# Expert weight loads that wait for the landing of the load three places ahead

## What is computed

```
def moe_swiglu(h, router, w1, w3, w2):
    logits = (h @ router).astype(jnp.float32)
    top_v, top_i = lax.top_k(logits, TOP_K)
    probs = jax.nn.softmax(top_v, axis=-1)
    gate = jnp.sum(jax.nn.one_hot(top_i, N_EXPERTS, dtype=jnp.float32) * probs[..., None], axis=-2)
    out = jnp.zeros(h.shape, jnp.float32)
    for e in range(N_EXPERTS):
        out = out + gate[..., e:e + 1] * swiglu(h, w1[e], w3[e], w2[e]).astype(jnp.float32)
    return out.astype(h.dtype)
```

## Time and profile before

| | us |
|---|---|
| median of 3 runs | 2490.42 |
| lowest and highest | 2488.22, 2502.24 |
| the profiled execution | 2504.0 |
| its span in the profile | 2502.2 |

### The profile page before, as it was taken

The page is one execution under the profiler, slowest core; times in us unless marked ns, Lnnn a source line. Parts: engine busy times, 40 slices in busy tenths (PEclk is TensorE's granted clock), DMA queues, the critical chain, the costliest instruction groups (busy, mean ns, idle before and its releaser), DMA issues. The chain is left out here.

```text
span 2502.2 us, 105337 instructions
## 1 busy us (share of the span) xinstructions
PE 2418.6 (97%) x46610; PEld 2015.9 (81%) x46610; DVE 1280.6 (51%) x3333; ACT 607.6 (24%) x1798; POOL 0.2 (0%) x4
## 2 busy tenths in 40 slices
PE   9999999999999999999999999999999999999987
PEld 8987666666699999998765666678999989888876
DVE  7566666666686776666575666677311111111111
ACT  2233333433311100233333333421111111111111
POOL 0000000000000000000000000000000000000000
PEclk9999999999999999999999999999999999999989
DMA  6334432222343454343343222236779999999986
GB/s 249 128 137 151 164 121 91 81 82 74 103 152 135 156 177 145 121 142 140 122 162 131 80 79 77 84 133 245 283 286 365 403 381 389 409 373 393 409 319 270
DMA packets 142657, 496.81 MB, mean 199 GB/s; under 512 B 18400, under 2 KB 23136, under 8 KB 139904
## 3 DMA queue, kind: packets, MB, share of 16 engines
q1 hardware_dynamic: 142336, 492.24, 53.5%
HBM read 471.88 MB, written 20.29 MB: 197 GB/s over the span
## 5 line engine op out<-in xcount | busy, mean ns | idle before, releaser
L306 PE MATMUL psum<-hT,ring 128*64 128x144 f32 (+1 forms) x4568 | 458.3, 346 | 3.4 <-DVE hT L2468 1.7
L306 PEld LDWEIGHTS psum<-hT,ring 128*64 128x64 f32 x4568 | 294.2, 137 | 95.1 <-issue 11.0
L2992 DVE TENSOR_TENSOR work<-psum,work 128x88 f32<-128x88 f32 (+3 forms) x176 | 42.4, 241 | 368.4 <-PE psum L2661 368.1
L2661 PE MATMUL psum<-work,ring 128*64 128x88 f32 (+3 forms) x5120 | 191.9, 234 | 10.2 <-issue 9.4
L2661 PEld LDWEIGHTS psum<-work,ring 128*64 128x64 f32 x5120 | 184.2, 138 | 15.3 <-issue 13.9
L1794 ACT ACTIVATE work<-psum 128x256 f32<-128x256 f32 (+4 forms) x320 | 104.1, 362 | 349.8 <-PE psum L1705 84.8
L306 PE MATMUL psum<-work 128*64 128x144 f32 (+4 forms) x2096 | 155.6, 283 | 4.3 <-DVE work L1285 3.6
L306 PE MATMUL psum<-y_ret,work 128*64 128x144 f32 x2400 | 156.2, 286 | 0.7 <-DVE y_ret L550 0.7
L306 PEld LDWEIGHTS psum<-y_ret,work 128*64 128x64 f32 x2400 | 148.7, 137 | 1.0 <-issue 1.0
L306 PEld LDWEIGHTS psum<-work 128*64 128x64 f32 (+2 forms) x2096 | 122.3, 136 | 31.1 <-issue 11.5
L2983 DVE TENSOR_TENSOR xT<-xT,psum 128x288 f32<-128x288 f32 x64 | 29.1, 455 | 229.4 <-PE psum L2701 228.4
(11 more groups left out here) (528 smaller groups left out, 4175.5 us busy)
## 6 DMA issues: line engine op xcount, KB each, us to landing
ring<-w_ff_dram SPq DMA_DIRECT2D x272, 512.0 KB, 8.2
ring<-w_mix_dram SPq DMA_DIRECT2D x256, 512.0 KB, 3.9
proj<-w_ff_dram SPq DMA_DIRECT2D x96, 512.0 KB, 9.8
lora_w<-w_ff_dram SPq DMA_DIRECT2D x64, 512.0 KB, 7.0
hT<-w_ff_dram SPq DMA_DIRECT2D x64, 512.0 KB, 7.3
y_ret<-w_ff_dram SPq DMA_DIRECT2D x64, 512.0 KB, 8.0
merged<-w_ff_dram SPq DMA_DIRECT2D x32, 512.0 KB, 10.6
work<-s_gla_dram SPq DMA_DIRECT2D x8, 1024.0 KB, 5.1
```

The lines of the kernel that those rows point to most:

```text
L306: last = nc.tensor.matmul(out[64 * c:64 * c + 64], weights[:, 64 * c:64 * c + 64], x, start=start, stop=stop)
L2661: last = mm(up_ps(s, cap)[64 * h:64 * h + 64], up_slot[s][:, k, 64 * h:64 * h + 64], hg[:, k, 0:cap], start=(k == 0), stop=(k == KT - 1))
L2992: tt(hid[:, f, 0:cap], up_ps(2 * f + 1, cap), act1[:, f % 2, 0:cap], ALU.mult).then_inc(sig("up_used"), 2)
```

## The change

In front of the wait for its place and its issue, each load gets a second wait: for the landing of the load three places ahead of it in SP's order (`UNDER_WAY = 3`), which may be one of the expert before. `landed` finds that load's semaphore and the count that it has to reach; for down places 4 and 9, whose semaphore is shared with the next place, it returns without a wait, and the load three places on goes out without one. `load_up` and `load_down` become one function. A `settle` (an increment of a semaphore that nobody waits for) stands between the two waits. `mixed_fills` moves up unchanged, since SP now uses it as PE does. What is loaded, its order, its places and all work of PE, ACT and DVE stay.

```diff
+        UNDER_WAY = 3
...
-            def load_up(p, e, n):
-                sp.wait_ge(slab_done, count(p, EX_SLABS, FF0 + n - EX_RING + 1 - (EX_DOWN if n < EX_RING else 0)))
-                sp.dma_start(up_slot[n % EX_RING], w_ff[e, n]).then_inc(up_in[n % EX_RING], 16)
-
-            def load_down(p, e, d):
-                sp.wait_ge(slab_done, count(p, EX_SLABS, FF0 + UP_SLABS + d - EX_RING + 1
-                                            - (UP_SLABS if d < EX_RING else 0)))
-                sp.dma_start(down_slot[d % EX_RING], w_ff[e, UP_SLABS + d]).then_inc(down_in[d % EX_RING], 16)
-
-            for n in range(EX_RING, UP_SLABS):
-                load_up((0, 0), 1, n)
-            for d in range(EX_RING, EX_DOWN):
-                load_down((0, 0), 1, d)
+            def landed(p, j):
+
+                if j < UP_SLABS:
+                    s, turn = j % EX_RING, j // EX_RING
+                    earlier = mixed_fills(s - 6) if s >= 6 else 0
+                    sp.wait_ge(up_in[s], count(p, UP_TURNS * 16, (earlier + turn + 1) * 16))
+                else:
+                    s, turn = (j - UP_SLABS) % EX_RING, (j - UP_SLABS) // EX_RING
+                    if s in DOWN_SHARED:
+                        return
+                    both = 2 if s in DOWN_SHARED.values() else 1
+                    earlier = mixed_fills(s - 1) if 6 <= s < 9 else 0
+                    nth = earlier + (turn + 1) * both
+                    sp.wait_ge(down_in[s], count(p, DOWN_TURNS * both * 16, nth * 16))
+
+            def load(i, done, e, j):
+
+                if j >= UNDER_WAY:
+                    landed((i, done), j - UNDER_WAY)
+                elif done:
+                    landed((i, done - 1), j - UNDER_WAY + EX_SLABS)
+                p = i, done
+                settle(sp)
+                if j < UP_SLABS:
+                    s = j % EX_RING
+                    sp.wait_ge(slab_done, count(p, EX_SLABS, FF0 + j - EX_RING + 1 - (EX_DOWN if j < EX_RING else 0)))
+                    sp.dma_start(up_slot[s], w_ff[e, j]).then_inc(up_in[s], 16)
+                else:
+                    s = (j - UP_SLABS) % EX_RING
+                    sp.wait_ge(slab_done, count(p, EX_SLABS, FF0 + j - EX_RING + 1
+                                                - (UP_SLABS if j < UP_SLABS + EX_RING else 0)))
+                    sp.dma_start(down_slot[s], w_ff[e, j]).then_inc(down_in[s], 16)
+
+            for j in itertools.chain(range(EX_RING, UP_SLABS), range(UP_SLABS + EX_RING, EX_SLABS)):
+                load(0, 0, 1, j)
...
-                for n in range(UP_SLABS):
-                    load_up((i, 1), e, n)
-                for d in range(EX_DOWN):
-                    load_down((i, 1), e, d)
+                for j in range(EX_SLABS):
+                    load(i, 1, e, j)
```

More of the change, by code:

```diff
@@ L10 @@
+import itertools
 from contextlib import ExitStack, contextmanager
@@ L2549, in up_ps, with mixed_fills @@
             return bank[UP_BANKS[n % EX_RING % len(UP_BANKS)]][:, 0:cap]
+        def mixed_fills(s):
+            return fills_before(layer, s) + fills(len(STREAM), s)
         def column_of(v, n):
@@ L2644, in gather_tokens @@
                     last.then_inc(sig("hg_ps"), 1)
-            def mixed_fills(s):
-                return fills_before(layer, s) + fills(len(STREAM), s)
             def up(p, cap, s, turn):
```

## The result

| | before | after |
|---|---|---|
| median, us | 2496.33 (4 runs) | 2696.90 (4 runs) |
| lowest and highest | 2488.22, 2514.48 | 2693.36, 2698.90 |
| span of the profiled execution | 2502.2 | 2693.5 |

The ratio is 1.0791, with a 95% interval from 1.0726 to 1.0856: slower, and by more than twice what was forecast. The median lies above the top of the range (2661). Most executions of the kernel before lie near 2489 us and some near 2503 us, the profiled one of 2504.0 among these; against a step of 190 us this does not matter.

What follows compares the result with a forecast made beforehand. In the later experts DMA and PE were both taken as near their limits. 456 x 1.51 + 6 x 6.6 = 728.2 us against 634.8 is +93.4, less 5.6 gives +88: 2578 us, 8 in 10 from 2484 to 2661.

Steps and rivals of the forecast that it cites:

- The form of the sum: In the experts, 462 slab landings: 456 at pace P and six at 6.6 us, 728.2 us against 634.8.
- P = 1.51: Forecast us per slab landing in the experts with three under way, the mean of 1.46 and 1.57.
- the two stretches of the earlier trace: 1916 to 1930 and 1829 to 1844 us, about four loads under way: 335 and 358 GB/s, 1.57 and 1.46 us a slab.
- Nearer to the upper row than the lower one: Placed the experts' pace, 1.51 us a slab, between a lower bound of 1.2 and an upper of 1.70.
- The reaction: SP's time from the landing of load j-3 to the issue of load j, estimated at 0.2 us.
- the bound of 1.70: Upper bound of the experts' pace, from one load landing after 4.9 us: (4.9 + 0.2)/3 = 1.70 us a slab.
- worse still: Rival: experts' pace at 1.70 us a slab, +171, 2661 us; top end of the slower case (0.70), holding little of it.
- The jumps: SP's loop jumping back at six expert borders: the queue runs dry, 6.6 us between two landings each, 39.6 in all.
- The tail: From last slab landing to end of the down products: 7.1 us now, some 1.5 needed, giving back 5.6 us.
- Three are enough: Rival: experts' queue stays full at 1.28 us a slab, 0 to 10 us added, 2490 to 2500 us; chance 0.13.
- The short queue frees the instruction loads: Rival: PE code comes sooner in the experts, half of 37.7 us of "issue" waits gone, 2476 us; chance 0.17.
- The sign posts: Trace signs in the experts: near 350 GB/s, landings 4 to 4.5 us, SP waiting on landings, PE idle about 5 us per jump.

Runs made afterwards that it cites:

- the half slabs: The changed kernel with two under way and each experts' load fetching only half its slab (256 KB): 2617.99 us, ratio 1.0511 to the kernel before.

## Why the prediction was wrong

**What bounds the kernel** was right. The PE with slabs at hand was not the limit, the added instructions on SP cost nothing beyond the turn (twelve under way shows it), and the loss is in the landings of 462 slabs.

**The form of the sum** was right too: a turn of landing and reaction, a third of it a slab, six jumps, and a PE that hides behind. With measured terms it is 456 x 1.747 + 28.7 = 825.3 us; this comes out by the way in which the pace is defined, and the test of the turn is that (4.94 + 0.30) / 3 gives the same 1.747.

**The step that failed** is the choice of the pace: P = 1.51, measured 1.747. It is 456 x 0.237 = 108 us of a miss. Three things are in it:
- The landing time with two others ahead. By P = 1.51 and 0.2 us of reaction it would be 4.3 us; it is 4.94. The difference, 0.61 / 3, is 0.20 of the 0.237. The right number was on record: the earlier trace rows, the only row with exactly the state that the change makes, said 4.9 us. I took it as an upper bound, from one load, and went by the two stretches of the earlier trace rows instead, because these showed ten loads on end. But they showed four under way (3.5 and 3.9 in the mean, worked out from the trace; in the changed kernel it is 2.8), and four have a pace of their own: 1.446 measured here, beside the 1.46 and 1.57 of these stretches. They would have done better as a forecast for UNDER_WAY = 4.
- "Nearer to the upper row than the lower one" was argued from bounds of which the lower could not be reached: 3.4 us is the landing of a load alone, and with two others under way it took 4.94. What adds these 1.5 us stays open: if only the bytes at 410 GB/s were shared, three would have been enough (last section).
- The reaction. 0.2 us was an estimate; it is 0.30 (median 0.295), and a `settle` and a second wait stand behind the wait for the landing. That is 0.033 of the 0.237, 15 us. With both ahead of that wait it is 0.15.

So also the bound of 1.70 was no bound: with the right reaction it is (4.9 + 0.30) / 3 = 1.73, and the rival "worse still", priced at 2661, would have been near 2676. It was the case that happened, and the range ended at its price, with no room for the terms in it.

**The jumps** were put at 6.6 us each, 39.6; they took 3.8 to 6.2, 28.7 in all, which gave back 10.9 us. In the one at 2196 us the issue of the expert's last two loads ended at 2196.4, and the next load was issued at 2201.98:

```profile
2194.41 1.95 SPq L2594 DMA_DIRECT2D merged<-w_ff_dram  x2
2201.98 1.01 SPq L2589 DMA_DIRECT2D lora_w<-w_ff_dram  x2
```

5.6 us, where it had been 7.2; over the six, 5.5 to 6.8 from issue to issue against 7.2 to 7.9. Why the jump itself is shorter was not tried. That the queue runs dry at each is right: at all six the last load had landed 0.5 to 2.0 us before the next was issued, and the one issued at 2201.98 landed after 3.26 us, somewhat sooner than the 3.6 of the one that found the queue empty in the earlier trace rows.

**The tail** was to give back 5.6 us and gave 3.1; the start, left out, cost 4.0, as the last loads of the first expert already waited.

**In sum,** +93.4 was forecast for the landings, +108.1 for the pace and -10.9 for the jumps come to it, which makes +190.6. The measured one is +190.5. So the miss is one of size, in the pace, and not of mechanism.

**The rivals.** "Three are enough" needed a landing in 3.6 us with two ahead; it took 4.9, so it is out. The Trainium skill ("DMA: Bandwidth & Descriptors", section "Anatomy of one DMA — SWDGE (gpsimd) path") gives about 2.0 us plus the bytes at 436 GB/s, for another issuing path than SP's, from which 3.2 us for a slab is an estimate. The trace agrees with it for a load alone (3.26 us in the chain), and not with others under way (4.2, 4.9, 5.4 and 6.1 us with two to five). "The short queue frees the instruction loads" did not show in any time, as told above. "Worse still" is what happened.

**The sign posts.** GB/s near 350 was wrong (292), a landing of 4 to 4.5 us wrong (4.9), SP waiting for landings and a chain of DMA pieces right. The PE idle for about 5 us at each jump was right only in part: around the six it idles for 2.9 to 5.5 us in all, mostly in two or more pieces, and only once for over 5 us in one. The PE's clock did fall more often: 0.94 from 2000 to 2100, where it had been 1.00; nothing of it is needed in the sum, since the landings alone account for it.

## What to carry to other kernels

Transfers from one queue whose number is limited by a wait run at number / (landing time + reaction), as long as that wait is the one that binds, and the landing time has to be that with just so many under way, not that of a load alone and not that of a full queue; for the 512 KB loads of this kernel five of them, 2.5 MB, reached the full rate (409 GB/s from 2225 to 2270 us), and with six no loss could be told any more. Where one row of a trace shows exactly the state that a change makes, its number goes into the sum, even if it is one load, and longer evidence from a neighbouring state goes into the range. And a range that ends at a rival's price needs room for the rival's own terms.

## What the runs showed of the hardware that was not expected

- The landing time of a 512 KB load rises slowly with the number under way: about 3.3 us alone (3.26 at a jump), 4.2 with two, 4.9 with three, 5.4 with four, 6.1 with five, 7.1 with six. In a queue that is full throughout each further load would add the 1.28 us of its bytes at 410 GB/s; the steps are 0.9, 0.7, 0.5, 0.7 and 1.0. So part of each transfer, some 1.6 us by the half slabs, runs beside the others without filling the engines. One piece of it shows in the changed kernel's trace: at the six jumps, with nothing else under way, the first packet starts 1.0 to 1.1 us after the issue. But if such a part were all, and the engines gave full rate behind it, three under way would land in 3 x 1.28 - 0.30 = 3.5 us and not in 4.9. Why they don't is open.
- The busy share hides this. After the change the engines are marked 0.86 busy at 294 GB/s, where in the kernel before 0.98 was marked in the same stretch; at the full queue's rate 294 of 410 is 0.72. Most 4 KB packets take as long as before (median 160 ns before, 159 now, from 1860 to 2440 us), but the mean rises from 166 to 190 ns (200 with two under way), because 9% of them are marked longer than 200 ns, where it was 1.6%. From 2225 to 2270 us, with ten loads under way, the kernel before has next to none of these.
- Stalls of the PE without a cause in the profile differ a good deal between profiles of kernels with the same PE work. The profiled execution of before has the wait of 7.5 us at the border at 2391.6, and a mean granted clock of 0.91 around it and 0.83 behind it:

```profile
2380.00:2400.00 20.00, 12.48 (x317) 10.76 (x315) 1.82 (x4) 3.09 (x9) 0.00 (x0) 0.91 0.77 294
2400.00:2420.00 20.00, 16.79 (x433) 16.55 (x431) 2.86 (x10) 1.62 (x7) 0.00 (x0) 0.83 0.79 277
```

  The clock had been at 0.91 from 2360 to 2380 already, ahead of this wait, so the wait is not what lowered it first. The profile with twelve under way has 6.4 us at the same border and a span of 2501.6; the one with six has no wait on "issue" over 2.4 us and a span of 2491.5. That such a stall makes up the difference is what these profiles suggest; it was not tested.
